# A hybrid mixer and sparse-expert block on one core: the mixer's loop on the engines takes three steps per turn

## The chip, the cores and the metric

One core of one Trainium2 chip runs the whole program. The metric is the device time of one execution in microseconds (us); lower is better. About 0.2% (7.4 us) is what a measurement of this kernel can tell from no change.

## What is computed

The input is a sequence of 4096 tokens of width 1024 (float32), with 16 learned tokens put in front. First a mixer with a residual, then a sparse mixture of experts with a residual, then a norm:

```python
h = concatenate([meta, x])
h = h + hybrid_mixer(rmsnorm(h, mix_norm), ...)     # w_in, two branches, w_out
h = h + hierarchical_moe(rmsnorm(h, ffn_norm), ...) # top-1 of 4 groups, top-2 of 8 experts in it
return rmsnorm(h, final_norm)[:, 16:]
```

The mixer projects each token to 3080 columns. 512 + 512 of them feed a gated linear recurrence (RG-LRU: a causal convolution of four taps, two gates from block-diagonal matrices, h = a*h + b over time, times a GeLU gate). The rest feed a gated delta rule with four heads of width 128, computed in chunks: a triangular system is solved within a chunk and a state of 128x128 per head goes from chunk to chunk. Both results, normed, go through w_out.

## The kernel before

The program has four phases, one after the other: constants and masks; the mixer with the router; a short phase that makes the tables of blocks; the experts in blocks of 128 tokens, and the final norm. Only the mixer phase is touched.

**Tiles and steps.** The mixer works on 33 tiles (TILES) of 128 tokens, all weights resident in SBUF. A step i does different stages for different tiles, so that the engines overlap: `Step` (L77) says that step i turns the input of tile i+2 (stage F), projects tile i+1 (P), runs both recurrences of tile i (G), multiplies tile i-1 by w_out (O) and routes tile i-2 (R). Each stage has a count of how often it has been done, for example `nG` = i+1 after this step and `pG` = i before it, and these counts are what the engines wait for: `need(eng, sem, value)` (L112) is a wait until a semaphore has reached a value such as `6 * s.pG + l - 1`.

**One program per engine.** Each of the five engines (SP, PE, ACT, DVE, POOL) has its own function `body(s)` with the operations of one step in an order written out by hand, and calls `steps(engine, body)` (L98). There is no barrier between steps: only the semaphores tie the engines together. `steps` writes the steps -2 to 3 out one after the other, with waits on constants. The steps 4 to 30 (LOOP = (4, 31), 27 steps) are one loop that each engine runs for itself, with i in a register: the counts are then computed in registers by the engine's sequencer, once each per turn. At the end of the body each sequencer adds 1 to its register, compares and branches back to the loop's first instruction; in the trace these stand at L103. The steps 31 to 34 are written out again.

**The order around the end of a step.** On PE a step ends with the products with w_out (`w_out_part`, L622 and L628), then L814 and L817 (sums of squares of k and q by a product with ones). The next step begins with the 24 products of `project(s, 0, 0)` (L569), then L674, L675 and L677 (the cumulated gates), 72 more of L569, products of the heads (L689, L694), turned k and v (L698, L703), 24 of L569, and L710, which needs the bank that ACT has emptied at L923 (`vt`). On ACT a step ends with L858/L860 (norms) and L1026, L1028 (the router's exponentials); the next begins with the load of an activation table (L883), L887 to L893 on four columns per head, and L858/L860 for k and q, which read what PE made at L814 and L817. Then come L904 (after DVE's L1248), L910, L913, L916 (after DVE's L1268), L854 and L923. On DVE a step ends with L1436 to L1440 (the router's gates) and the next begins with L1223, L1227 (needs ACT's L893), L1230, L1232 to L1242, L1246, L1248, L1260, L1268.

Of the kernel before, what the change touches and what calls it, by code (L numbers as in the profile page):

```python
# [68 lines left out]
U_SCALE = 512.0  # L69
W_TOP = 16384.0  # L70
LOOP = (4, TILES - 2)

def bcast(ap, shape):
# [24 lines left out]
def steps(eng, body):  # L99

    for i in range(-2, LOOP[0]):
        body(Step(i))
    with eng.Fori(LOOP[0], LOOP[1]) as i:  # L103
        body(Step(i))
    for i in range(LOOP[1], TILES + 2):
        body(Step(i))

# [7 lines left out]
def hymba_block(nc, xm, w_in, w_out, conv_w, lru_cols, w_r, w_i, mix_g, ffn_g, final_g, dn_g, dn_a,  # L115
                dn_dt, w_router, b_router, w_gate, w_up, w_down, out):
    with ExitStack() as ctx:
# [363 lines left out]
        with nc.Block() as block:  # L481
            @block.sync
            def _(sp):
# [4 lines left out]
                def body(s):  # L488
# [15 lines left out]
                    if s.O:  # L504
# [5 lines left out]
                        if isinstance(s.i, int) and s.i == TILES - 1:  # L510

                            sp.wait_ge(sem("ba_full"), TILES)
                            for slot in range(WSLOTS):
                                load_expert(sp, slot, slot)
                steps(sp, body)
                sp.wait_ge(sem("h_stored"), 16 * (TILES - 1))
                sp.wait_ge(sem("u_stored"), 32 * (TILES - 1))

            @block.tensor
            def _(pe):  # L520
# [137 lines left out]
                def body(s):  # L658
# [151 lines left out]
                    if s.P:  # L810
# [5 lines left out]
                        need(pe, sem("lrs_ln"), s.nG)  # L816
                        pe.matmul(flat(bA), ones[:], flat(rnq), start=True, stop=True).then_inc(sem("nq_full"), 1)  # L817
                steps(pe, body)

            @block.scalar  # L820
            def _(act):
# [53 lines left out]
                def body(s):  # L875
# [147 lines left out]
                    if s.R:  # L1023
# [3 lines left out]
                                             accum_out=rsm[:, 2:3]).then_inc(sem("exp_ready"), 1)  # L1027
                        nc.scalar.activation(rsm[:, 3:4], rsm[:, 1:2], ACT.Exp).then_inc(sem("exp_ready"), 1)  # L1028
                steps(act, body)

            @block.vector
# [908 lines left out]
```

## Time and profile before

| | |
|---|---|
| median of 3 runs | 3720.98 us (3719.39 to 3726.59) |
| the profiled execution's own time | 3717.44 us |
| its span, first to last instruction | 3715.8 us |
| mean granted TensorE clock | 0.955 |
| PE busy over the span | 3323.3 us (89%) |
| loop of the mixer (27 steps), by PE's L817 | 443.42 to 2374.52 us |

Columns of the rows that the prediction quotes: the timeline gives start, length, engine, line, operation, output<-inputs, shape and count of merged instructions, and in square brackets the idle time ahead with what ended it. The rows by line give count, then minimum/median/maximum in ns, then the first and last start in us; an engine's name with a q is its sequencer. The rows of waits give the waiting operation, what released it, us in total, how often, and the longest. "issue" is idle time in which the engine waited for nothing that the profile shows.

### The profile page before, as it was taken

The page shows a single profiled execution, that of the slowest core. Times are in us where ns is not written, and L with a number is a line of the kernel's source. Part 1 is how long each engine was busy: PE and PEld are TensorE (multiplying, and loading weights), DVE is VectorE, ACT ScalarE, POOL GpSimd, SP SyncE. Part 2 cuts the span into 40 slices and gives each one's busy share as a digit, 9 for nine tenths or more (in the row PEclk, how much of TensorE's full clock was granted, in tenths as well). Part 3 has the DMA queues.
Part 4 walks back from the last instruction along what each step waited for, and adds up shares of the span by engine and source line. Part 5 has one row for each costly group of instructions (what it writes and reads, how often), then busy time and mean ns, then how long its engine had stood idle before and what let it go on. Part 6 is the DMA issues. An engine that isn't in the chain of part 4 may idle for free. (4 is left out here: it accounts for less than half of the span.)

```text
span 3715.8 us, 81902 instructions
## 1 busy us (share of the span) xinstructions
PE 3323.3 (89%) x29622; PEld 2487.9 (67%) x29623; DVE 2202.1 (59%) x6137; ACT 1504.3 (40%) x3145; POOL 810.3 (22%) x859
## 2 busy tenths in 40 slices
PE   3888999999999999999999999984999999999900
PEld 2887888888788788878878878852444454444400
DVE  5786777777777677777777767753222222222267
ACT  4454544544554454454455445432111111111168
POOL 2322221212222122121222212211111111111065
PEclk8899999999999999999999999986999999999955
DMA  5000111110111111111011111131665544546299
GB/s 204 7 7 18 36 47 36 36 47 30 36 47 36 36 36 47 36 36 47 30 36 47 36 36 36 41 159 67 227 232 192 192 158 158 192 165 230 103 361 379
DMA packets 94472, 362.53 MB, mean 98 GB/s; under 512 B 16081, under 2 KB 16210, under 8 KB 81874
## 3 DMA queue, kind: packets, MB, share of 16 engines
q1 hardware_dynamic: 49330, 219.35, 16.1%
q0 software_dynamic: 26032, 77.69, 5.9%
q10 hardware_dynamic: 18800, 60.64, 4.0%
q8 instruction: 282, 4.62, 0.6%
q14 instruction: 28, 0.23, 0.0%
HBM read 246.45 MB, written 111.18 MB: 96 GB/s over the span
## 5 line engine op out<-in xcount | busy, mean ns | idle before, releaser
L569 PE MATMUL pj<-uT,W 128*128 128x128 f16 x15840 | 978.2, 220 | 29.0 <-issue 29.0
L569 PEld LDWEIGHTS pj<-uT,W 128*128 128x128 f16 x15840 | 933.6, 98 | 79.3 <-issue 73.7
L1698 PE MATMUL bA<-W,uT 128*128 x1328 | 588.7, 596 | 6.6 <-issue 4.0
L1698 PEld LDWEIGHTS bA<-W,uT 128*128 128x128 f32 x1328 | 248.1, 192 | 288.3 <-issue 288.3
L1785 DVE TENSOR_TENSOR W<-W,bA 128x256 f32<-128x256 f32 x83 | 34.9, 421 | 562.9 <-ACT W L1732 562.9
L1685 PE MATMUL pj<-W 128*128 x664 | 298.8, 593 | 1.8 <-ACT W L1737 1.8
L644 PE MATMUL bA<-dec,Mt 128*128 128x128 f32 x1584 | 222.7, 284 | 15.9 <-DVE dec L1203 14.1
L655 PE MATMUL bB<-X,qh 128*128 128x128 f32 x1584 | 222.6, 284 | 3.3 <-ACT qh L871 3.3
L1732 ACT ACTIVATE W<-bA 128x256 f32<-128x256 f32 x83 | 31.9, 384 | 463.5 <-PE bA L1698 463.5
L644 PEld LDWEIGHTS bA<-dec,Mt 128*128 128x128 f32 x1584 | 193.1, 192 | 23.6 <-DVE dec L1203 21.4
L1685 PEld LDWEIGHTS pj<-W 128*128 128x128 f32 x664 | 119.9, 190 | 121.5 <-issue 121.5
L655 PEld LDWEIGHTS bB<-X,qh 128*128 128x128 f32 x1584 | 194.5, 194 | 4.7 <-ACT qh L871 4.7
L1523 POOL DMA_INDIRECT idx_tab<-toki,posi x64 | 64.5, 1007 | 608.5 <-DVE posi L1409 542.1
L586 PE MATMUL pj<-W,uT 128*128 128x512 f16 x792 | 191.5, 379 | 0.0
L871 ACT ACTIVATE qh<-bA 128x256 f32<-128x256 f32 x198 | 77.1, 389 | 278.8 <-PE bA L644 276.3
L628 PE MATMUL bO<-W,yl 128*128 128x512 f16 x768 | 183.3, 382 | 0.0
L1720 ACT ACTIVATE W<-pj 128x512 f32<-128x512 f32 x83 | 49.7, 599 | 329.1 <-PE pj L1685 329.1
L628 PE MATMUL bO<-W,yt 128*128 128x512 f16 x768 | 178.1, 378 | 0.0
L1502 POOL TENSOR_TENSOR yg<-hh,gg 128x512 f32<-128x512 f32 x33 | 42.0, 1273 | 588.1 <-DVE yl L1346 569.3
L1197 DVE COPY_PREDICATED X<-lvl,bB 128x256 f32<-128x256 uint8 x165 | 81.9, 496 | 117.3 <-PE bB L655 108.7
L1760 DVE COPY W<-pj 128x512 f32<-128x512 f32 x83 | 57.4, 692 | 156.0 <-PE pj L1685 156.0
L1658 POOL DMA_INDIRECT x_in<-u_rows,gid x42 | 41.1, 978 | 396.6 <-PE bO L1675 369.2
(407 smaller groups left out, 6068.0 us busy)
## 6 DMA issues: line engine op xcount, KB each, us to landing
y_rows<-W ACTq DMA_DIRECT2D x83, 512.0 KB, 3.1
W<-w_gate SPq DMA_DIRECT2D x32, 1024.0 KB, 6.7
W<-w_up SPq DMA_DIRECT2D x32, 1024.0 KB, 9.9
W<-w_down SPq DMA_DIRECT2D x32, 1024.0 KB, 11.9
x_in<-xm SPq DMA_DIRECT2D x33, 512.0 KB, 3.6
ht<-xm SPq DMA_DIRECT2D x32, 512.0 KB, 3.6
h_rows<-ht SPq DMA_DIRECT2D x32, 512.0 KB, 2.6
u_rows<-ht SPq DMA_DIRECT2D x32, 512.0 KB, 3.8
```

The source lines that it names most:

```text
L569: mm = pe.matmul(pj[g % 2][:, j, :], w16[:, k, w_half(w_high, COL[GROUPS[g]], 512, j * P, P)], (ul if low_u else uh)[:, k, :], start=(k == ...
L586: mm = pe.matmul(flat(pj[1]), u[:, k, :], w16[:, k, w_half(w_high, c, 512)], start=(k == 0 and n_pass == 0), stop=(k == KT - 1 and n_pass ...
L628: mm = pe.matmul(bOf[:, 512 * half:512 * half + 512], y, wo16[:, j, w_half(w_high, 512 * half, 512)], start=(j == 0 and not w_high), stop= ...
L644: mm = pe.matmul(bA[:, h, :], Mt[:, h, :], T[:, h, :], start=True, stop=True)
L655: mm = pe.matmul(bB[:, h, :], Y[:, h, :], X[:, h, :], start=True, stop=True)
L871: nc.scalar.activation(first_half(Y, l), first_half(bA, l), ACT.Copy).then_inc(sem("Y_new"), 1)
L1197: a = nc.vector.copy_predicated(second_half(X, l), mask_of(l), second_half(bB, l))
L1523: pool.indirect_dma_start(out=idx_tab, out_offset=bass.IndirectOffsetOnAxis(ap=posi[:, a:a + 1], axis=0), in_=toki[:], in_offset=None).the ...
L1685: mm = pe.matmul(flat(pj[half]), hm2[:, j, :], w[:, j, 512 * half:512 * half + 512], start=(j == 0), stop=(j == 1))
L1698: mm = pe.matmul(bA[:].rearrange("p a b -> p (a b)").rearrange("p (g f) -> p g f", g=2), xT[:, k, :], w[:, k], start=(k == 0), stop=(k == ...
L1720: nc.scalar.activation(yo[par][:, 0:512], flat(pj[0]), ACT.Copy).then_inc(sem("yo_a"), 1)
L1760: nc.vector.tensor_copy(yo[par][:, 512:D], flat(pj[1])).then_inc(sem("yo_b"), 1)
```

## The change

`steps` makes a turn of the loop out of three steps. The register now counts turns, n = 0 to 8, and the three copies of the body get i = 3n+4, 3n+5 and 3n+6. The order of the operations within a step, the steps ahead of the loop and those behind it are the same.

```diff
 LOOP = (4, TILES - 2)
+TURN = 3
...
     for i in range(-2, LOOP[0]):
         body(Step(i))
-    with eng.Fori(LOOP[0], LOOP[1]) as i:
-        body(Step(i))
+    with eng.Fori(0, (LOOP[1] - LOOP[0]) // TURN) as n:
+        for k in range(TURN):
+            body(Step(TURN * n + (LOOP[0] + k)))
     for i in range(LOOP[1], TILES + 2):
         body(Step(i))
```

## Rows read from the trace of the kernel before

**Rows 1.** The page, part 1: busy us (share), instructions.
```profile
PE 3323.3 (89%) x29622; PEld 2487.9 (67%) x29623; DVE 2202.1 (59%) x6137; ACT 1504.3 (40%) x3145; POOL 810.3 (22%) x859
```

**Rows 2.** Stretches: 26 steps with a back edge, step 4, step 3; clock, DMA share last.
```profile
514.50:2374.52 1860.02, 1820.02 (x21009) 1546.98 (x21008) 1368.79 (x4265) 931.02 (x2055) 404.33 (x364) 1.00 0.11 38
443.42:514.50 71.08, 70.20 (x810) 59.68 (x809) 52.58 (x164) 35.71 (x80) 15.53 (x14) 1.00 0.12 39
373.02:443.42 70.40, 70.03 (x809) 59.61 (x808) 52.27 (x163) 35.26 (x80) 15.64 (x14) 1.00 0.11 39
```

**Rows 3.** Waits of PE, 514.5 to 2374.52 us.
```profile
PE pj L569 <- issue: 29.0, 26, 1.4
PE pj L622 <- ACT zs L1005: 6.2, 26, 0.2
PE bA L644 <- DVE dec L1203: 4.8, 26, 0.2
```

**Rows 4.** Timeline of PE across one back edge.
```profile
1086.73 1.02 PE L817 MATMUL bA<-rnq,ones 128*128 128x512 f32 x2
1088.86 1.34 PE L569 MATMUL pj<-uT,W 128*128 128x128 f16 x21 [1.11 <-issue]
```

**Rows 5.** The same on the way into the loop, step 4, no branch back.
```profile
443.42 1.02 PE L817 MATMUL bA<-rnq,ones 128*128 128x512 f32 x2
444.28 1.50 PE L569 MATMUL pj<-uT,W 128*128 128x128 f16 x24
...
455.84 1.16 PE L710 MATMUL bC<-St,kh 128*128 128x128 f32 x8 [0.36 <-ACT vt L923]
```

**Rows 6.** ACT's L923, which L710 needs: step 4, and a step behind a back edge.
```profile
455.20 0.59 ACT L923 ACTIVATE vt<-bC 128x512 f32<-128x512 f32 x1
```
```profile
1098.84 0.59 ACT L923 ACTIVATE vt<-bC 128x512 f32<-128x512 f32 x1
```

**Rows 7.** Line 103, the loop's branches by sequencer, 27 each.
```profile
L103 POOLq COMPARE_BRANCH  x27: 40/45/58, 503.2 to 2363.2; - x27
L103 PEldq COMPARE_BRANCH  x27: 83/3645/3895, 512.7 to 2372.8; - x27
L103 ACTq COMPARE_BRANCH  x27: 40/45/63, 513.2 to 2373.2; - x27
L103 DVEq COMPARE_BRANCH  x27: 50/56/74, 514.5 to 2374.6; - x27
```

**Rows 8.** DMA queues that carry instructions: in the loop, 514.5 to 2374.5 us.
```profile
q8 instruction: 233, 3.82, 1.0%
```

**Rows 9.** The same in written-out steps, 300 to 443 us.
```profile
q8 instruction: 13, 0.21, 0.7%
q14 instruction: 5, 0.04, 0.1%
```

**Rows 10.** Line 103, one back edge of ACT and of DVE.
```profile
L103 ACTq COMPARE_BRANCH  x1: 45/45/45, 1085.4 to 1085.4; - x1
```
```profile
L103 DVEq COMPARE_BRANCH  x1: 56/56/56, 1086.8 to 1086.8; - x1
```

**Rows 11.** Timeline of ACT, then of DVE, across that back edge.
```profile
1085.75 0.19 ACT L1028 ACTIVATE rsm<-rsm 128x1 f32<-128x1 f32 x1
1085.95 1.28 ACT L883 ACT_TABLE_LOAD   x1
```
```profile
1087.96 0.16 DVE L1227 SCALAR_TENSOR_TENSOR g<-al,ga 128x4 f32<-128x4 f32 x1 [0.48 <-ACT ga L893]
```

**Rows 12.** Line 112, register and semaphore operations of ACT and DVE, one step.
```profile
L112 ACTq ALU_OP  x20: 35/35/38, 1016.1 to 1085.8; - x20
L112 ACTq EVENT_SEMAPHORE  x16: 17/17/38, 1018.3 to 1084.7; - x16
L112 ACTq FUSED_REGOPS  x8: 37/37/37, 1019.5 to 1086.0; - x8
```
```profile
L112 DVEq ALU_OP  x20: 40/40/45, 1015.7 to 1081.2; - x20
```

**Rows 13.** Timeline of PE after its longest stall ahead of the loop.
```profile
226.36 2.04 PE L817 MATMUL bA<-rnq,ones 128*128 128x512 f32 x2 [9.31 <-ACT lrs L858]
228.19 2.62 PE L569 MATMUL pj<-uT,W 128*128 128x128 f16 x24
```

## The prediction

> **What bounds the kernel now.** I read the page first, then the stretches of the loop, then PE's waits in it, then the branches at L103 on each sequencer. The page says that PE is the busiest engine by far [rows 1]. In the 26 steps that follow a back edge PE is busy 1820 of 1860 us, and its clock is granted in full [rows 2]: a step lasts 1860.02/26 = 71.54 us and PE sets it. The 40 us left are almost all named: 29.0 us of "issue" ahead of L569, once per back edge, 1.1 us each, and two small waits of 0.2 us each per step [rows 3]. So the loop's back edge is the only hole in PE that this change can touch.
>
> Across a back edge the first L569 starts 2.13 us after L817 (1088.86 - 1086.73) [rows 4]; into step 4, with no branch back, it starts 0.86 us after (444.28 - 443.42) [rows 5]. The edge thus costs PE 1.27 us where it stands. Its cause is in the branches: PE's takes 3.65 us in the median and up to 3.90, against 0.08 for the one that leaves the loop, while those of ACT, DVE and POOL take 0.05 us in all 27 cases [rows 7]. Most of PE's 3.65 us is covered by the products already queued. The DMA rows say why. In the loop the queue q8 carries 233/26 = 9 packets of instructions a turn, 147 KB; q14 carries none [rows 8]. In written-out steps q8 carries 6.5 a step, and q14 has five packets of 8 KB in two steps [rows 9]. I read this so: q8 is PE's own queue, and PE fetches its body anew in every turn, with the first instructions of the body only after the branch; the others keep their short bodies, so q14 falls silent. ACT's body is 80 operations and some 46 for registers, semaphores and the branch per step, DVE's 164 and some 90 (counted between two branches; the larger parts are in [rows 2, 12]): some 126 and 256 instructions. The program now stands at 26 back edges; the change makes them 8.
>
> **The change, part by part.**
>
> *Eighteen back edges go.* At first sight 18 x 1.27 = 22.9 us. But step 4 is what a step without a back edge is: same registers, full set of stages, same order. It lasts 71.08 us [rows 2], only 71.54 - 71.08 = 0.46 us less. The rest comes back as a wait: PE reaches L710 early and waits 0.36 us for ACT's L923 [rows 5]. L923 starts 11.78 us after L817 there (455.20 - 443.42) and 12.11 us after it behind a back edge (1098.84 - 1086.73) [rows 6]. So the chain through the start of a step on ACT and DVE (table load L883, L887 to L893, DVE's L1227 to L1268, then L916, L854, L923) ends at nearly the same time either way, and it is late next. It bounds the gain: 18 x 0.46 = 8.3 us.
>
> *The body triples.* PE's edge misses already and stays as it is. DVE's body becomes some 760 instructions, ACT's some 370, POOL's 84. The trace before shows no body of ACT or DVE larger than 126 and 256, so whether they still stay is not shown. DVE with 256 instructions stays, PE with 1657 does not. Thirteen packets of 16 KB for two written-out steps of 1657 PE instructions [rows 9] are 255 instructions a packet, so one of q14's 8 KB holds some 128: DVE's body grows from 2 or 3 such blocks to 6 or 7, ACT's from 1 or 2 to 3 or 4. I take it that both will now run through more blocks than are kept, and that their branch will wait as PE's does. Price of such a branch, D: not below 0 extra, since the present one is 0.05; a gain is excluded, as the branch is there before and after. At most PE's 3.90 us [rows 7]. I take 3.0: PE's 3.65 less half of one packet's time, since q14's packets are half the size of q8's; a q8 packet takes 1.0% x 16 x 1860/233 = 1.28 us [rows 8], half of it 0.64.
>
> *Where this wait lies.* ACT's branch starts at 1085.4 and the table load L883 at 1085.95, 0.2 us after the start of L1028 [rows 10, 11]; with a branch of 3.0 us L883 starts about 2.9 us later. DVE's branch starts at 1086.8 and L1227 at 1087.96, having waited for ACT [rows 10, 11]; its own 3.0 us run beside ACT's and end sooner than ACT's L893 then does, so the delays are not added. Behind L883 stands the chain above, which has no slack in a step without an edge, so PE's L710 comes 2.9 us later, and the step. PE's own 1.27 us is covered by it. Queued behind: on ACT L887 onwards, on DVE L1223 onwards and through g4 POOL's L1472 and PE's L674.
>
> *Registers.* Each count is now computed from 3n instead of i. Such an operation takes 0.035 us on ACT and 0.040 on DVE, 28 and about 20 of them a step at L112 [rows 12]. I cost them at nothing: they run while the engine is busy. If the cover is gone, as ahead of L883, two or three more give 0.1 us x 27 = 2.7 us. Below zero is possible too, since neighbouring steps share counts; -1 us.
>
> *SP and POOL.* Their sequences are short and idle most of the time (POOL 404 of 1860 us [rows 2]); a missed branch of 3 us there is hidden: POOL's is over 12 us ahead of its next work. Costed at nothing; cover gone, POOL's L1472 is late and costs what ACT's delay costs.
>
> **The sum.** The loop now: 71.08 + 26 x 71.54 = 1931.1 us, as L817 says (2374.52 - 443.42). After: 27 x 71.08 + 8 x D = 1919.2 + 8 x 2.9 = 1942.4 us. Difference +11.3 us, on the profiled execution's 3717.44 us (span 3715.8) 3728.7. The median of the runs stands 3.5 us above that execution, so I forecast 3720.98 + 11.3 = 3732.3, rounded 3732. The sign turns at D = 11.9/8 = 1.5 us.
>
> A rule stands beside the point on which this hangs. The trace shows PE missing at each turn with 1657 instructions, and DVE hitting with 256 [rows 7, 8]. The Trainium skill, "Runtime: NRT & Kernel Launch", Instruction fetch mechanics, says that the instruction memory holds 512 instructions for most engines and 2048 for PE, and that a taken branch whose target is outside the window waits for a DMA. By size alone PE's present body would fit, and the trace does not agree: 3.65 us. For the new bodies the size rule would let DVE miss and ACT hit, which is the third case below.
>
> **The rivals.**
>
> *Both engines hit (ends faster).* ACT and DVE keep their longer bodies. For it: no miss of theirs in the trace before [rows 7]. Against it: PE's body is refetched whole [rows 8]. Then 27 x 71.08 + 8 x 0.46 = 1922.8 us, -8.3 us: 3712.7. It decides wherever D stays under 1.5 us.
>
> *The full hole comes back.* As above, but ACT's L923 also comes earlier in steady running, so each edge is worth 1.27: -22.9 us, 3698. Against it: the wait at L710 in step 4 and 0.33 us of shift in L923 [rows 5, 6].
>
> *Only DVE misses.* DVE's branch starts at 1086.8, ends 3.0 us later, and with the 0.7 us of registers, L1223 and semaphores between it and L1227, that starts at 1090.5 instead of 1087.96: D = 2.5. 27 x 71.08 + 20 - 1931.1 = +8.1 us: 3729.
>
> *PE's clock falls at each edge.* PE would now be idle some 2 to 3 us near each edge. After 9.31 us of idling L817 took 2.04 us for two and L569 2.62 us for 24 [rows 13], against 1.02 and 1.50 [rows 5]. That would add 2.1 us x 8 = 17 us: +28, 3749. For it: only that the idle time grows; against it: 1.1 us holes leave the clock at 1.00 [rows 2].
>
> *It does not do what it says.* (31-4)/3 = 9 turns with no remainder, the same 27 steps. If the registers of three steps cost more than sharing saves, steps grow by the 0.1 us above; that is inside the range.
>
> **How the numbers follow.** Forecast (ACT and DVE both miss) 0.64: D from 2.0 to 3.9 gives +4 to +19 us, with registers 3724 to 3743. Both hit 0.16; full hole 0.06; only DVE 0.07; clock 0.07. The range 3710 to 3743 leaves out the full hole, the clock, and tails of some 0.05. The bound of 0.2% is 7.4 us, 3713.5 and 3728.4. Slower: 0.57 of the forecast's 0.64, 0.04 of only DVE, 0.07 clock: 0.68. Faster: 0.09 of both hit (its -8.3 is just past the bound), 0.06: 0.15. Same: 0.17. The forecast's own range is 3724 to 3743.
>
> **What would show it.** L103 nine times per sequencer; ACT's and DVE's branch at about 3000 ns in eight of nine; PE's still near 3650. q14 in the loop: some ten packets of 8 KB a turn. PE's "issue" 8 times instead of 26; L710 waiting 0.36 us for L923 in some 18 steps, and waits of PE on ACT or DVE near L674 to L710 of 2 to 3 us in 8. Steps by L817: 71.1 us inside a turn, 74.0 us after an edge. Branches of 0.05 us on ACT and DVE would prove me wrong, and so would steps of 70.3 us inside a turn.

## The result, and the profile after

The changed kernel takes 3729.98 us in the median of nine runs (3726.25 to 3734.01), the kernel before 3720.37 in nine runs taken beside them. The ratio is 1.0027 [1.0016, 1.0037]: 9.6 us more, where 11.3 were forecast. The profiled execution of after took 3734.01 us (span 3732.4, clock 0.953), 16.6 more than the one of before; it is the slowest of its nine, so the two traces show more than the medians differ by. One of the six executions of e12 below took 9342.51 us, in a state of its own: it counts in that kernel's median and not in its ratio.

By PE's L819 (before: L817) the loop runs from 444.93 to 2388.69 us, 1943.8 us against 1931.1: +12.7. Another 1.5 us lie ahead of the loop and 2.4 behind it; they come back below.

The page's first part, and then stretches of one step each from L819 to L819: step 4, the last step of the first turn, the three of the second turn, and the two slowest steps behind a back edge. The columns are those of [rows 1] and [rows 2].

```profile
PE 3342.2 (90%) x29622; PEld 2502.4 (67%) x29623; DVE 2204.4 (59%) x6137; ACT 1500.4 (40%) x3145; POOL 809.0 (22%) x859
```

```profile
444.93:516.20 71.27, 70.20 (x810) 59.68 (x809) 52.77 (x165) 35.80 (x80) 15.51 (x14) 1.00 0.11 39
587.53:658.53 71.00, 70.20 (x810) 59.70 (x809) 52.61 (x165) 34.85 (x79) 15.52 (x14) 1.00 0.11 39
658.53:731.85 73.32, 70.58 (x809) 59.64 (x808) 52.77 (x165) 36.46 (x80) 15.53 (x14) 1.00 0.11 38
731.85:803.23 71.38, 70.21 (x810) 59.70 (x809) 52.64 (x165) 35.64 (x80) 15.52 (x14) 1.00 0.11 38
803.23:874.23 71.00, 70.20 (x810) 59.70 (x809) 52.61 (x165) 34.83 (x79) 15.51 (x14) 1.00 0.11 39
874.23:948.83 74.60, 72.02 (x810) 60.90 (x809) 52.76 (x165) 36.58 (x80) 15.59 (x14) 0.98 0.11 38
1091.21:1167.65 76.44, 73.28 (x809) 62.13 (x808) 52.84 (x165) 36.67 (x80) 15.59 (x14) 0.96 0.11 37
```

The pattern of the second turn (73.3, 71.4, 71.0) holds for all but these two steps. The 19 steps with no edge ahead last 71.19 us in the mean, six of the eight behind an edge 73.36, and the other two 74.60 and 76.44. Compared with 71.54 for a step of before, the 18 edges that went gave back about 6.3 us and the eight that stayed cost 591.2 - 8 x 71.54 = 18.9 us more.

Waits of PE in the loop of after, which answer to [rows 3], then one wait each of ACT and of DVE in the same stretch. Before, ACT had no such wait, and DVE one of 0.43 us per edge (11.2 us in 26) at L1223:

```profile
PE pj L571 <- issue: 10.4, 8, 2.7
PE bA L646 <- DVE dec L1205: 8.0, 26, 0.5
PE bC L712 <- ACT vt L925: 7.4, 24, 0.4
PE pj L624 <- ACT zs L1007: 6.0, 25, 0.2
PE bC L679 <- POOL dec L1474: 4.2, 7, 0.6
PE bT L676 <- DVE g L1232: 2.0, 5, 0.7
```

```profile
ACT L885 <- issue: 18.1, 8, 2.8
```

```profile
DVE rxc L1225 <- issue: 24.2, 8, 3.2
```

PE's hole at the edge is still there and has become rarer, 10.4 us instead of 29.0. What is new is that ACT stands still for 18.1/8 = 2.26 us and DVE for 3.0 us at each edge that is left, both with nothing to wait for that the profile shows. Behind that PE waits for DVE (L676), for POOL (L679) and for ACT (L712).

The branches themselves, by line, to be held against [rows 7]; then the sequencers of ACT and DVE at one edge ([rows 10]):

```profile
L104 PEldq COMPARE_BRANCH  x9: 83/3610/5083, 656.8 to 2386.9; - x9
L104 ACTq COMPARE_BRANCH  x9: 40/45/63, 657.2 to 2387.4; - x9
L104 DVEq COMPARE_BRANCH  x9: 60/68/74, 658.6 to 2388.8; - x9
```

```profile
L104 ACTq COMPARE_BRANCH  x1: 63/63/63, 657.2 to 657.2; - x1
L104 DVEq COMPARE_BRANCH  x1: 74/74/74, 658.6 to 658.6; - x1
L104 ACTq MOVE  x1: 29/29/29, 659.8 to 659.8; - x1
...
L104 DVEq FUSED_REGOPS  x1: 80/80/80, 661.5 to 661.5; - x1
```

ACT's branch is over in 0.06 us, and the next thing that its sequencer does, the MOVE at the same line, comes 2.6 us after the branch began; on DVE it is 2.9 us. Before, and in the kernels below that leave the body of one of them at one step, it is 0.23 us on ACT and 0.30 on DVE (0.28 and 0.36 at the first edge). So both miss, that is, they have to fetch the start of their body again: four of q14's packets start between 658.2 and 662.1 us. The wait does not stand in the branch's own record, as PE's does: it stands behind it, and the gap shows it.

What it does to the engines, in the timelines of PE, ACT and DVE across the same edge ([rows 4, 11]):

```profile
658.53 1.02 PE L819 MATMUL bA<-rnq,ones 128*128 128x512 f32 x2
660.62 1.51 PE L571 MATMUL pj<-uT,W 128*128 128x128 f16 x24 [1.07 <-issue]
662.41 0.39 PE L676 MATMUL bT<-g,tri 128*128 128x4 f32 x2 [0.28 <-DVE g L1232]
...
663.62 1.12 PE L679 MATMUL bC<-dec,ones 128*128 128x512 f32 x2 [0.61 <-POOL dec L1474]
...
673.18 1.16 PE L712 MATMUL bC<-St,kh 128*128 128x128 f32 x8 [0.36 <-ACT vt L925]
```

```profile
657.54 0.19 ACT L1030 ACTIVATE rsm<-rsm 128x1 f32<-128x1 f32 x1
659.89 1.28 ACT L885 ACT_TABLE_LOAD   x1 [2.17 <-issue]
...
672.54 0.59 ACT L925 ACTIVATE vt<-bC 128x512 f32<-128x512 f32 x1
```

```profile
658.46 0.17 DVE L1442 COPY saved<-rt 128x6 f32 x1
661.68 0.21 DVE L1225 TENSOR_SCALAR rxc<-xst,rdsc 128x1 f32<-128x1 f32 x1 [3.05 <-issue]
```

L925 starts 672.54 - 658.53 = 14.01 us after L819. It was 12.11 behind an edge of before and 11.78 with no edge [rows 6], and the step grew by the same 2.2 us over one without an edge (73.32 against 71.08 for step 4 of before).

The queues of instructions in the loop of after ([rows 8]):

```profile
q8 instruction: 181, 2.97, 0.7%
q14 instruction: 111, 0.91, 0.2%
```

q14, silent before, carries 111 packets of 8 KB: 7 in what the window holds of the first turn and 13 in each of the eight others.

The two slowest steps have a second cause. PE at the third edge, then at the second, and last 10 us from near the second and from near the third (the clock is the third number from the end):

```profile
1091.21 1.02 PE L819 MATMUL bA<-rnq,ones 128*128 128x512 f32 x2
1094.97 2.60 PE L571 MATMUL pj<-uT,W 128*128 128x128 f16 x24 [2.74 <-issue]
```

```profile
876.10 1.51 PE L571 MATMUL pj<-uT,W 128*128 128x128 f16 x24 [0.85 <-issue]
878.30 0.39 PE L676 MATMUL bT<-g,tri 128*128 128x4 f32 x2 [0.69 <-DVE g L1232]
...
879.52 1.52 PE L679 MATMUL bC<-dec,ones 128*128 128x512 f32 x2 [0.60 <-POOL dec L1474]
880.83 3.36 PE L571 MATMUL pj<-uT,W 128*128 128x128 f16 x34
```

```profile
877.50:887.50 10.00, 8.70 (x93) 7.58 (x91) 8.82 (x20) 6.07 (x15) 6.02 (x5) 0.83 0.04 13
1094.90:1104.90 10.00, 9.93 (x101) 8.71 (x102) 7.78 (x17) 4.92 (x12) 6.01 (x5) 0.66 0.01 3
```

At the third edge PE's branch took 5.08 us, PE stood still for 2.74 us, and the 24 products behind it took 2.60 us instead of 1.51: for part of these 10 us the clock was granted at 1.2 GHz. At the second edge the branch took 3.38 us as usual, and the idle times of 0.85, 0.69 and 0.60 us ahead of L571, L676 and L679 came before a clock of 0.83. Together the two steps are 4.3 us longer than two of the other six. Of the nine runs the three with a mean clock of 0.953 took 3733.7 to 3734.0 us and the six with 0.956 or 0.957 took 3726.3 to 3731.8: stretches at half clock in some runs and not in others would explain much of the spread, but only this one run of the nine was traced.

### The profile page after: what moved, and what is told of

It is laid out like the page before. It is cut to its first block and busy times, and to the rows that moved or that the text cites. A ratio compares the mean times of both kernels' runs of the same rounds, so it can differ in the third digit from the quotient of the medians.

```text
span 3732.4 us, 81407 instructions
## 1 busy us (share of the span) xinstructions
PE 3342.2 (90%) x29622; PEld 2502.4 (67%) x29623; DVE 2204.4 (59%) x6137; ACT 1500.4 (40%) x3145; POOL 809.0 (22%) x859
## 5 line engine op out<-in xcount | busy, mean ns | idle before, releaser
L571 PE MATMUL pj<-uT,W 128*128 128x128 f16 x15840 | 983.3, 220 | 10.4 <-issue 10.4
L571 PEld LDWEIGHTS pj<-uT,W 128*128 128x128 f16 x15840 | 940.3, 99 | 57.7 <-issue 52.1
L646 PE MATMUL bA<-dec,Mt 128*128 128x128 f32 x1584 | 225.4, 286 | 19.5 <-DVE dec L1205 17.7
L646 PEld LDWEIGHTS bA<-dec,Mt 128*128 128x128 f32 x1584 | 195.5, 194 | 27.2 <-DVE dec L1205 25.0
L1199 DVE COPY_PREDICATED X<-lvl,bB 128x256 f32<-128x256 uint8 x165 | 81.9, 496 | 121.5 <-PE bB L657 112.9
L1474 POOL TENSOR_TENSOR dec<-tri,g 128x512 f32<-128x512 f32 x33 | 34.2, 1035 | 442.4 <-DVE g L1232 442.4
```

The source lines that it names most:

```text
L571: mm = pe.matmul(pj[g % 2][:, j, :], w16[:, k, w_half(w_high, COL[GROUPS[g]], 512, j * P, P)], (ul if low_u else uh)[:, k, :], start=(k == ...
L646: mm = pe.matmul(bA[:, h, :], Mt[:, h, :], T[:, h, :], start=True, stop=True)
L1199: a = nc.vector.copy_predicated(second_half(X, l), mask_of(l), second_half(bB, l))
```

## Experiments

All kernels but the changed one share this helper, so that each engine can be given its own number of steps per turn (1 is the kernel before, 27 means that no loop is left):

```diff
-def steps(eng, body):
+def steps(eng, body, turn=1):
...
+    if turn == LOOP[1] - LOOP[0]:
+        for i in range(*LOOP):
+            body(Step(i))
+    elif turn == 1:
+        with eng.Fori(LOOP[0], LOOP[1]) as i:
+            body(Step(i))
+    else:
+        with eng.Fori(0, (LOOP[1] - LOOP[0]) // turn) as n:
+            for k in range(turn):
+                body(Step(turn * n + (LOOP[0] + k)))
```

The lines of these kernels stand 8 to 10 below those of before. "Loop" is steps 4 to 30 by the sum of squares of q, 1931.1 us before. The ratios are to runs of before taken beside each group, whose medians were 3714.04 us (e1 to e4), 3719.66 (e5 to e8) and 3716.47 (e9 to e12), so kernels of different groups compare by their ratios. The times of loops and steps come from one traced execution each. What was expected of each stands in front of what follows from it; here is what all of them gave:

| kernel | median us | ratio to before | loop us |
|---|---|---|---|
| e1: PE alone three steps per turn | 3711.92 | 0.9992 [0.9982, 1.0002] | 1930.0 |
| e2: ACT and DVE three, PE one | 3734.82 | 1.0055 [1.0041, 1.0069] | 1950.6 |
| e3: all nine | 3708.98 | 0.9989 [0.9980, 0.9998] | 1925.3 |
| e4: all written out | 3696.93 | 0.9951 [0.9937, 0.9965] | 1912.5 |
| e5: ACT alone three | 3731.57 | 1.0033 [1.0023, 1.0043] | 1945.7 |
| e6: DVE alone three | 3735.63 | 1.0045 [1.0028, 1.0062] | 1948.7 |
| e7: loop from step 5, ACT alone two | 3700.99 | 0.9949 [0.9932, 0.9966] | 1918.0 |
| e8: before, with a prefetch hint on PE's branch | 3712.23 | 0.9977 [0.9967, 0.9987] | 1919.2 |
| e9: before, PE's loop head at the start of a block | 3705.34 | 0.9966 [0.9953, 0.9979] | 1919.3 |
| e10: before, `vt` (L923) emptied ahead of `xb` (L854) | 3715.46 | 0.9998 [0.9990, 1.0007] | 1929.9 |
| e11: e10 with the loop from step 5 | 3699.54 | 0.9948 [0.9935, 0.9961] | 1914.6 |
| e12: e10, all written out | 3694.68 | 0.9937 [0.9925, 0.9950] | 1909.5 |

### Which engine's longer body costs the time (e1 to e6)

```diff
-                steps(pe, body)
+                steps(pe, body, 3)
```

> Only PE's loop takes three steps per turn; SP, ACT, DVE and POOL branch back after every step. Theory A (what the changed kernel loses lies at the back edges of ACT and DVE, whose longer bodies are fetched anew): here ACT and DVE keep short bodies, so q14 is silent in the loop, PE branches back 8 times, steps inside a turn last about 71.1 us, those behind PE's edge 71.5 us, the loop of 27 steps (by PE's L817) 1923 us against 1931 before, ratio 0.998. Theory B (the loss comes from computing the counts from 3n, or from the traffic of instruction fetches): PE still has both, so the loop stays at 1931 us or above, ratio 1.000 to 1.002.

With PE's body alone tripled, steps 5 to 30 without an edge last 71.05 to 71.09 us and six of the eight behind one 71.2 to 71.65. ACT and DVE pick up 0.23 and 0.30 us after their branches began, and q14 is silent. Waits of PE in its loop:

```profile
PE pj L577 <- issue: 11.2, 8, 2.6
PE bC L718 <- ACT vt L931: 6.9, 19, 0.4
```

Without ACT's and DVE's longer bodies the loop is not slower. In the trace it isn't as fast as expected either: two edges cost 74.55 and 76.09 us, with branches of PE of 5.01 and 4.73 us and the clock at half behind them. Without these two the loop would be some 8 us shorter, near the 1923 expected. In both branches, and in the 5.08 us one of after, two packets of q8 were under way at once, the earlier of them 0.2 to 0.3 us ahead of the other, each taking 1.7 to 2.4 us; in the ordinary branches one packet of 0.9 to 1.5 us was. What delays these fetches is open. The traced execution is the slowest of the eleven (3720.80 us against a median of 3711.92), so its two slow edges do not tell of the others. Over the eleven the gain of PE's part cannot be told from nothing: 0.9992 [0.9982, 1.0002], where 0.998 was expected.

```diff
-                steps(act, body)
+                steps(act, body, 3)
...
-                steps(dve, body)
+                steps(dve, body, 3)
```

> Only ACT's and DVE's loops take three steps per turn; PE branches back after every step as before. Theory A: 8 of 26 edges also have a miss of ACT and DVE of 2.5 to 2.8 us, which hides PE's; those steps last about 73.4 us (more where PE's clock falls), the other 18 stay at 71.5 us; loop 1931 + 8 x 1.9 = 1946 us or a little above, ratio 1.004 to 1.006, worse than the full change. Theory B: the steps grow by 0.2 us each wherever they stand in the turn, about 5 us in all, ratio 1.001 to 1.002. If PE's own edge were what matters, ratio 1.000.

The loop grows by 19.5 us with PE's 26 edges left in place: the whole loss of the change, and more, comes from these two bodies. Steps behind an edge of ACT and DVE last 73.35 to 73.57, two of them 74.5, with 3.4 us at half clock in each of these.

> All engines take nine steps per turn: 2 back edges instead of 8 or 26, every body three times as long again. Theory A: 27 x 71.15 + 2 x 2.5 = 1926 us for the loop, -5 us against before, ratio 0.998 to 0.999. Theory B: as many registers from 9n and more blocks to fetch than with three steps, so no better than the change: ratio 1.002 or above.

Nine steps per turn on all five engines leave two back edges, of 73.27 and 73.43 us. The price of an edge does not grow with the body. With two edges in place of eight the traced loop is 5.8 us shorter than before's; the 0.1% by which the kernel is ahead is less than the 0.2% that can be told from no change.

> The 27 steps are written out on every engine, with waits on constants: no back edge and no count in a register. Theory A: steps as inside a turn but without registers, between 70.4 us (step 3 of the kernel before, written out) and 71.1 us; loop 1901 to 1920 us, ratio 0.992 to 0.997. Were straight-line fetching by itself costly, the steps would be above 71.5 us and the ratio over 1.000.

With no back edge, steps last 70.8 us, less than the 71.08 of step 4, and the loop is 18.6 us shorter. PE waits 7.7 us in 26 steps for L931 (before: L923), so the chain that bounded the prediction's gain is still what stands in the way.

e5 and e6 make one of the two lines of e2's diff each.

> Only ACT takes three steps per turn; DVE's body stays at one step. Theory A with both delays beside each other, not added: 8 gaps of 2.5 to 2.8 us on ACT behind its branch, none on DVE, PE's branches as before; the steps behind them last about 73.3 us, as with both engines; loop 1931 + 8 x 1.8 = 1945 us, ratio about 1.004. If it were DVE's miss that costs, the loop stays at 1931 us.

> Only DVE takes three steps per turn. Theory A: 8 gaps of 2.7 to 2.8 us on DVE behind its branch, none on ACT; L1227 of the kernel before starts some 2.4 us later, the steps behind the edges last about 73.2 us; loop 1944 us, ratio about 1.0035. If ACT's miss alone is what costs, the loop stays at 1931 us.

Each alone makes the step behind an edge nearly as long as both do at full clock: 73.13 to 73.41 us with ACT's body, 73.11 to 73.38 with DVE's, 73.2 to 73.6 with both (after, e2). Counted from the end of the branch, ACT's sequencer picks up after 2.46 to 2.71 us in e5 and DVE's after 0.25; in e6 it is 2.74 to 2.99 for DVE and 0.19 for ACT. The delays run side by side and meet at L1227, as the prediction had it: at the first edge of e5 DVE waits there 2.79 us for ACT, and at that of e6 not at all. e5's row of q14, then e6's:

```profile
q14 instruction: 42, 0.34, 0.1%
```

```profile
q14 instruction: 67, 0.55, 0.1%
```

Both windows also hold a few packets of the first turn. In each of the other turns there are 5 packets for ACT's 357 instructions (as counted between two branches of after) and 8 for DVE's 757. That would be the blocks of 128 that the body touches, 4 and 7, and one more. The two add up to the 13 a turn of after.

### Why PE misses and what keeps a body (e7 to e9)

```diff
-LOOP = (4, TILES - 2)
+LOOP = (5, TILES - 2)
...
-                steps(act, body)
+                steps(act, body, 2)
```

> The loop runs over the 26 steps 5 to 30, and ACT alone takes two steps per turn: some 250 instructions, as many as DVE's body of one step, which stays. If what stays goes by the count of instructions, ACT's branches (12 of them) are followed by the next register operation within 0.2 us and q14 is silent in the loop; steps 71.5 us, time as before (one back edge less on every engine, -0.5 us). If any body longer than one step is lost, the 12 edges cost 1.8 us each, +22 us, ratio 1.006.

ACT with 242 instructions stays (0.2 us behind its branch). The surprise is PE, whose body is the same: its branches take 0.21 us instead of 3.65, and q8 carries 6 packets in the loop, all in its first turn, instead of 233. All that had changed for PE was that one more step is written out ahead of its loop and one less is in it, so that the body starts elsewhere. Two kernels, each with another loop in the helper's branch for one step per turn, take that apart.

```diff
+HINTED = (mybir.EngineType.PE,)
...
+    elif turn == 1:
+        with eng.bass.Fori(LOOP[0], LOOP[1], engines=OrderedEngineSet([eng.engine]), hint_back_edge=eng.engine in HINTED) as i:
+            body(Step(i))
```

```diff
+    elif turn == 1:
+        head = {eng.engine: 0} if eng.engine == mybir.EngineType.PE else None
+        with eng.bass.Fori(LOOP[0], LOOP[1], engines=OrderedEngineSet([eng.engine]), head_slot=head) as i:
+            body(Step(i))
```

> The kernel before with one thing changed: PE's loop begins at the first instruction of a fetch block instead of somewhere in it (padding ahead of the loop). Theory C, from the run in which the loop began one step later and PE suddenly fetched nothing in the loop: what counts is how many blocks the body touches, and PE's 1657 instructions touch 7 blocks of 256 from here and 8 from where they stood. Then q8 falls silent in the loop, PE's branch takes 0.2 us instead of 3.65, the step 71.07 us; loop 1919 us, ratio 0.995 to 0.998. If the one step less, ACT's two steps per turn or the hint were what did it, this run is like the kernel before: q8 9 packets a turn, 71.5 us, ratio 1.000.

Here only the place of PE's loop head is chosen: the first slot of a block of 256 instructions. Branches by line (the 28th of PE is the jump to that slot ahead of the loop) and PE across one edge:

```profile
L109 PEldq COMPARE_BRANCH  x28: 76/208/321, 444.7 to 2364.0; - x28
L109 ACTq COMPARE_BRANCH  x27: 40/45/63, 516.2 to 2364.5; - x27
```

```profile
1086.19 1.02 PE L827 MATMUL bA<-rnq,ones 128*128 128x512 f32 x2
1087.05 1.50 PE L579 MATMUL pj<-uT,W 128*128 128x128 f16 x24
```

The hole is gone from every edge, q8 and q14 are both silent, and the steps last 71.07 to 71.10 us, step 4's 71.08 of before. The same 1657 instructions are kept or lost by where they begin. 1657 instructions touch 7 blocks of 256 if they start with one, and 7 or 8 otherwise; before, 9 packets a turn are 8 blocks and one more. That a body stays while its blocks and the one fetched ahead are at most 8 on PE, and at most 4 of 128 instructions on ACT and DVE, is what all runs agree with (DVE's 256 over 2 or 3 stay, ACT's 357 over 4 do not). The count is inferred from the packets, not shown: for PE only the first slot and two unknown places (e7, e8) against the place of before were run, and a rule of the loop head's slot by itself would fit these as well. Nor did any run move the head of ACT's 357, which from the first slot would touch three blocks and, by this count, stay.

The Trainium skill, "Runtime: NRT & Kernel Launch", Instruction fetch mechanics, gives room for 512 instructions on most engines and 2048 on PE; this is 4 blocks of 128 and 8 of 256, and in whole blocks the runs agree with it. Read by size alone it fails twice: ACT's 357 miss in e5, and PE's 1657 miss before and hit in e9. The page's block of 16 KB is not what ACT and DVE fetch here: q14's packets hold 8 KB.

### What is late next (e10 to e12)

```diff
-                    evac(s, 0, "xb")
                     if s.G:
                         need(act, sem("vt_full"), s.nG)
                         need(act, sem("vn_full"), s.pG)
                         nc.scalar.activation(vt[:], bC[:], ACT.Copy).then_inc(sem("vt_ready"), 1)
+                    evac(s, 0, "xb")
+                    if s.G:
...
```

> The kernel before, with ACT emptying the bank for vt ahead of the one for the recurrence's input, so that the vt that L710 waits for in a step without a stall is there some 0.6 us sooner. Theory A's point that PE's edge of 1.27 us and ACT's chain run beside each other: behind each of PE's 26 edges L710 doesn't wait for vt, so nothing is gained: ratio 1.000, step 71.5 us. If vt sets the step there too, steps fall by up to 0.4 us and the ratio to 0.997.

> The loop begins at step 5 on all engines, one step per turn, so that PE's body stays (no misses anywhere), and ACT empties vt first. Theory A: with the edge's stall gone the wait of 0.3 to 0.4 us at L710 is what is left, and this order takes most of it: steps 70.7 us instead of 71.05, loop 27 x 70.7 = 1909 us, ratio 0.991 to 0.994. If L710's wait only moves on, steps stay at 71.05 and the ratio at 0.995.

> The 27 steps written out on all engines, and vt first on ACT. Theory A: steps of 70.8 us fall by the 0.3 us of the wait at L710 to 70.5 us, loop 1903 us, ratio 0.990 to 0.994. If the wait only moves on, 70.8 us and 0.995 as without the new order.

In e10 nothing comes of it, since PE is late at the edge itself. In e11 PE's wait for `vt` is gone and the steps last 70.92 us, 0.16 less than in e9, not the 0.4 that was expected; e12 has 70.70 us, 0.1 less than e4, where 70.5 was expected. Waits of PE in e12:

```profile
PE pj L630 <- ACT zs L1014: 6.5, 27, 0.2
PE bA L652 <- DVE ot L1318: 5.7, 25, 0.6
```

The new wait for DVE's L1318 (before: L1309), 5.9 us in e11, takes the place of the one for ACT. e12 has the lowest ratio of all, 0.9937; e11, which keeps a loop of one step per turn, comes within 0.11% of it, and the intervals of e4, e7, e11 and e12 overlap.

## Why the prediction was right, and where it was not

The sign, the mechanism and the time came out: 3732 forecast, 3729.98 measured. The loop was forecast at 1942.4 us and took 1943.8, but that it came within 1.4 us is luck: two errors of 4 to 5 us meet.

- **ACT and DVE miss with the longer bodies.** Right, and e5 and e6 show it for each alone; "Only DVE misses" is out by e5, where ACT's body of 357 instructions is fetched in each turn. "Branches of 0.05 us on ACT and DVE would prove me wrong" was the wrong sign to look for: they did take 0.05 us, and the wait lies behind the record. What told was q14, which was forecast at some ten packets a turn and carried 13. The waits of PE of 2 to 3 us on ACT or DVE near L674 to L710 did not come in one piece either: at the first edge they are 0.28, 0.61 and 0.36 us behind 1.07 us of "issue". And DVE's delay does not end sooner than ACT's, as the prediction had it: at L1227 (after: L1229) it is the later one at about half of the eight edges.
- **D.** Taken as 2.9 us from PE's 3.65 less half a packet. It measured 2.26 at ACT's L885 and 73.36 - 71.08 = 2.28 in the step. The term is 8 x 0.6 = 5 us too large. No run shows the reason given for the 3.0, that a packet of half the size saves half a packet's time.
- **The clock.** The rival "PE's clock falls at each edge" had 0.07; it came true at two edges of eight in this execution, for 4.3 us and not 17, and in e3, e5 and e6 at none of 18. That PE would be idle for 2 to 3 us near each edge was seen; that this is enough now and then was not. It nearly fills in what D had too much. Without it the loop would be 8.4 us longer than before, not far from the 9.6 between the medians.
- **Steps with no edge.** Forecast at 71.08, measured 71.00 in the third step of a turn and 71.36 in the second. In the third the wait at L710 is 0.29 us instead of 0.36; this smaller wait is also found in e4 and in the second of ACT's two steps in e7, so it goes with a step that is not the first of one of ACT's turns. In the second PE waits 0.5 us at L646 for DVE's L1205 instead of 0.2 (8.0 us in 26 steps against 4.8). The nineteen steps with no edge come to 19 x 0.106 = 2.0 us more. It appears only where DVE's body is longer (after, e2, e3, e6), not in e5 or e1. In the second step of the second turn DVE's L1199 (before: L1197) starts 0.46 us after the record of its wait ended, in the third step 0.10 us, with nothing in between that the profile shows; what holds it is open.
- **The wait at L710.** Forecast in 18 steps, found in 24: behind an edge too, as all of ACT's chain is later. "The full hole comes back" is out by this row. The wait is no hard floor: it is shorter in e4 (0.29 us), and when ACT's order is changed (e11, e12) it is gone and part of it comes back as one for DVE.
- **PE's own edge.** "PE's edge misses already and stays as it is" held here, but the reason given for it, the size of the body, does not explain the miss of before: in e9 the same 1657 instructions stay. The limit on the gain was right for the same step either way, 71.08.

The sum of the loop again, with measured terms: 27 x 71.08 + 2.0 + 8 x 2.28 + 4.3 = 1943.7. These terms are read off the steps themselves, so this shows that nothing is left over, and no more. The 1.5 us ahead of the loop and 2.4 behind are hardly of the change. Ahead of it the first L819 comes 2.0 us earlier, two of the written-out steps are 3.9 us longer together and one 0.4 us shorter, with a stretch at half clock of 13.7 us instead of 10.2; e1 and e9 have the same lengths there and e2 and e5 those of before, though the steps ahead of the loop are the same in all. Behind it the kernels range over 1336.8 to 1344.8 us.

## What to carry over

Before a loop is partly unrolled, look at each engine's own branch, at what its sequencer does next, and at the queue of its instruction packets. Here an engine whose body is kept pays some 0.2 us a turn and has nothing to gain. The sequencer of one whose body is not kept stands still for 2.5 to 5 us a turn, with one, three or nine steps in it, of which 0.46 us reached the step on PE and 2.3 us on ACT or DVE. So try first to move the loop's head: one slot placement gave 0.34% here, where three steps per turn lost 0.27%. All steps written out gave 0.49%; unrolling by three only the engine that missed anyway (e1) gave nothing that could be told from no change.

## What the runs showed that was not expected

- A body of 1657 instructions on PE is fetched anew in each turn (9 packets of 16 KB, branch 3.65 us) or not at all (0.21 us); in e9 the place of its first slot is all that was changed.
- A missed branch shows in PE's record (3.3 to 3.9 us) but behind ACT's and DVE's (2.5 to 2.8 and 2.7 to 3.1 us from its end to the sequencer's next operation in e2, e5 and e6, with records of 0.04 to 0.07).
- Two packets of q8 in flight together at a branch of PE go with 4.7 to 5.1 us (e1, after); one with 3.3 to 3.9.
- Three holes of PE of under 1 us each came ahead of a stretch at 1.2 GHz at one edge of after (0.85, 0.69 and 0.60 us) and at two of e2 (0.81 or 0.84, 0.69, 0.59). Nearly the same holes (0.77, 0.76, 0.59) at a third edge of e2, and 1.07, 0.28 and 0.61 at the first of after, left the clock at 2.4 GHz. What decides it is open.
